# A decoder layer with 32 experts: 50 matrix products into an unread PSUM bank, between the output projection and the first expert

## The chip, the cores and the metric

The kernel runs on one NeuronCore of one Trainium2 chip. The metric is the device time of one execution in microseconds (us), the median of the runs shown. The engines are named as the profile names them: PE is TensorE (PEld its weight loads), DVE is VectorE, ACT is ScalarE, POOL is GpSimd, SP is SyncE. SP does no arithmetic here; it issues the large transfers from memory.

## The reference

One layer on 512 tokens of width 1024, float32:

```
p   = rmsnorm(x, g_mix) @ w_in          # q, k, v and three convolution inputs
mix = concat(rmsnorm(window_attention(q, k, v)), rmsnorm(short_conv(...)))
x   = x + mix @ w_out                   # the output projection
h   = rmsnorm(x, g_ffn)
logits = h @ w_router + b_router        # 32 experts; the top 4 of each token are used
act = clamped_swiglu(h[rows of expert e] @ w1[e] + b1[e])    # w1[e]: 1024 x 2048
y   = act @ w2[e] + b2[e]                                    # w2[e]: 1024 x 1024
x   = x + sum over the 4 experts of gate * y
out = rmsnorm(x, g_final)
```

The weights of the 32 experts are 12 MiB each in float32. They are all read once.

## The kernel before, in words

The 512 tokens are four tiles (t = 0 to 3) of 128. The work before the experts keeps them as rows or as columns of 128x128 blocks; the experts then take up to 96 rows each, gathered from memory by an index list (a "big" block: 64 rows at full width, 32 more as four quarters; `KINDS`, line 48, says which of the 32 places are big; places 0 and 1 are).

**The order of PE's work** is written out by hand in one list (lines 744 to 762 and on), and PE executes it strictly in that order; each step waits for semaphores of other engines. The stretch that matters here is:

- `out_proj(t, n)` (line 681): the output projection of tile t, column half n, into banks 0 and 1 (even t) or 2 and 3 (odd t). DVE adds the result to X in `residual` (line 1125).
- `turn_h2(t)` (line 707): eight 128x128 transposes of X into banks 4 and 5 (recorded at line 523, the helper's). ACT copies bank 4 to SBUF and DVE bank 5 (`turned_h2`, lines 1554 and 1146).
- `router(t)` (line 716): the logits, eight products of 32 columns that the trace shows as 16 instructions (line 728), into bank 6 or 0. DVE's `select(t)` (line 1151) takes the top four and marks the chosen experts.
- `rank(t)` (line 732): counts, for each token, how many earlier tokens chose the same expert. After `rank(3)` DVE's `place` (line 1173, timed at line 1184) compares ranks for the first two experts, and 16 products of one column (line 768) give the token lists of experts 0 and 1. DVE turns these to integers (line 1216), and POOL's indirect transfer fetches expert 0's rows (`fetch`, lines 1786 to 1789).
- Lines 772 and 773 count the tokens of each expert; DVE sorts the experts by count; lines 775 to 777 (after `sort_ready`) spread the order over partitions; lines 779 and 780 (after `nb_ready`) make prefix sums for overflow blocks.
- `turn_block(0)` (line 804) waits for expert 0's rows and transposes them (`turn_lines`, line 786). ACT copies them to `rowsT` (line 1603). Then `expert_blocks(compute)` runs the 32 experts.

DVE, ACT and POOL have hand-written orders of their own. DVE's order in this stretch is: select(0), select(1), residual(3,1), turned_h2(2), second_norm(3), place(0,2), turned_h2(3), select(2), select(3), place(2,4), the integer lists, the gates, the sort, the copies, and `list_entries` (line 1253). When `list_entries` is done, POOL writes the sorted list of all rows to memory by 16 indirect transfers (line 1814), reads it back (lines 1819 to 1821), and from it fetches the rows of expert 2 and every later one (line 1780).

**An expert** (`compute(i)`, line 899) is on PE: `first_product(i)` (w1, line 884: eight bias products on lines 834 and 837, then line 846 for the 64 rows and line 853 for the four quarters, in two groups of four slots), then, for i = 1, `turn_act_of(0)`, then `turn_block(i + 1)`, then `second_product(i - 1)` (w2, lines 859 to 878), then `turn_act_of(i)`. So `turn_block(2)`, which needs expert 2's rows, stands ahead of expert 0's second product. Every product reads its weights from a ring of 16 slots of 1 MiB.

**SP's order** fills the ring: eight loads of 2 MiB early (`load_first`, lines 450 to 465, the last one after expert 0's rows are in), then one load after another, each waiting (`wait_free`, line 430) until PE has used up the slots that it overwrites. The first of these needs the first group of expert 0's first product done; the w1 loads of place 3 need the first half of expert 0's second product.

`bias_sel` (96 x 2 x 128) and `bias_split` (96 x 3072), both bfloat16, are the operands of the bias products. `B_BOTH` (line 256) is bank 1.

Of the kernel before, what the change touches and what calls it, by code (L numbers as in the profile page):

```python
# [74 lines left out]
def layer_kernel(nc, x, g_mix, w_in, conv_w, sinks, g_attn_out, g_conv_out, w_out,  # L75
                 g_ffn, w_router, b_router, w1, b1, w2, b2, g_final, out):
    ctx = ExitStack()
    with ctx:
        def sb(name, shape, dt=F32):
            return ctx.enter_context(nc.sbuf_tensor(name, shape, dt))  # L80
# [5 lines left out]
        def sem(name):  # L86
            return ctx.enter_context(nc.semaphore(name))
# [42 lines left out]
        bias_split = sb("bias_split", [3 * E, 2 * FF + D], BF16)  # L130
        expert_sel = sb("expert_sel", [3 * E, E], BF16)
        bias_sel = sb("bias_sel", [3 * E, 2, P], BF16)
# [57 lines left out]
        ps = ctx.enter_context(nc.psum_tensor("ps", [P, 8, 512], F32))  # L190
# [65 lines left out]
        B_GLU, B_BOTH, B_LIN, B_Y, B_T = 0, 1, 2, 4, 6  # L256
# [11 lines left out]
        consts_ready, alibi_ready, biases_ready = sem("consts_ready"), sem("alibi_ready"), sem("biases_ready")  # L268
# [27 lines left out]
        cur_copied, cur_ready = sem("cur_copied"), sem("cur_ready")  # L296
# [43 lines left out]
        def fetches(upto):  # L340

            return 16 * sum(2 if BIG[i] and i >= STATIC else 1 for i in range(upto + 1))
# [7 lines left out]
        def expert_blocks(run):  # L350

            for i in range(E):
                run(i, i % 2)
# [163 lines left out]
        def _(pe):  # L517
            mm = pe.matmul

            def turn_rows(src, bank):  # L520

                for k in range(KT):
                    ins = pe.transpose(ps[:, bank + k // 4, (k % 4) * P:(k % 4 + 1) * P],
                                       src[:, k * P:(k + 1) * P], ident[:, :])
                return ins
# [155 lines left out]
            def out_proj(t, n, amid=None):  # L681

                if n == 0:
                    pe.wait_ge(mix_lo, t + 1)
                elif t == 0:
                    pe.wait_ge(wout_lo, KT)
                pe.wait_ge(x2_half, n * TB + t - 1)
                for k in range(KT):
                    if amid and k == CT:
                        amid()  # L690
                    bank, high, low, w_high, w_low = out_parts(t, n, k)
                    mm(bank, high, w_high, start=(k % CT == 0), stop=False)
                    mm(bank, high, w_low, start=False, stop=False)
                    ins = mm(bank, low, w_high, start=False, stop=(k % CT == CT - 1))
                ins.then_inc(oproj_done, 1)
# [11 lines left out]
            def turn_h2(t):  # L707
                pe.wait_ge(x2_half, TB + t + 1)
                if t == 0:
                    pe.wait_ge(gstd_ready, 1)  # L710
                else:
                    pe.wait_ge(h2T_a, t)
                    pe.wait_ge(h2T_b, t)
                turn_rows(X[:, t, :], 4).then_inc(h2_turned, 1)

            def router(t):

                pe.wait_ge(h2T_a, t + 1)
                pe.wait_ge(h2T_b, t + 1)
                if t == 0:  # L720
                    pe.wait_ge(wrt_ready, 1)
                elif t == 1:
                    pe.wait_ge(x2_half, 2 * TB - 1)
                else:
                    pe.wait_ge(chosen_ready, t - 1)
                logits = ps[:, LOGIT_BANKS[t % 2], 0:E]
                for k in range(KT):
                    ins = mm(logits, xnT[:, k, t * P:(t + 1) * P], w_rt[:, k, :],
                             start=(k == 0), stop=(k == KT - 1))
                ins.then_inc(logits_done, 1)  # L730

            def rank(t):

                pe.wait_ge(chosen_ready, t + 1)
                if t == 0:
                    pe.wait_ge(consts_ready, 2)
                if t == 2:
                    pe.wait_ge(pick_ready, 2 * t)
                own = ps[:, 7, t * E:(t + 1) * E]
                ins = mm(own, earlier[:, :], chosen[:, t, :], start=True, stop=(t == 0))  # L740
                if t:
                    ins = mm(own, ones_bf[:, :], chosen_cum[:, t, :], start=False, stop=True)
                ins.then_inc(rank_done, 1)
# [6 lines left out]
            out_proj(1, 1)  # L750
            turn_h2(0)
            out_proj(2, 1, lambda: router(0))
            turn_h2(1)
            out_proj(3, 1, lambda: router(1))
            turn_h2(2)
            router(2)
            rank(0)
            rank(1)
            turn_h2(3)
            router(3)  # L760
            rank(2)
            rank(3)

            pe.wait_ge(pick_ready, 2 * TB)
            for e in range(2):
                for t in range(TB):
                    for part in range(2):
                        ins = mm(ps[:, 5, e:e + 1], pick[:, e, t, :], tok_value[:, t, part:part + 1],
                                 start=(t == 0 and part == 0), stop=(t == TB - 1 and part == 1))
            ins.then_inc(tok_summed, 1)  # L770

            mm(ps[0:E, 4, 0:1], chosen_cum[:, TB, :], ones_bf[:, 0:1], start=True, stop=True)
            mm(ps[0:E, 4, E:2 * E], ones_bf[:, 0:E], chosen_cum[:, TB, :], start=True, stop=True).then_inc(counts_done, 1)
            pe.wait_ge(sort_ready, 1)
            mm(ps[0:1, 5, 2 * E:3 * E], expert_no[:, :], in_place[:, :], start=True, stop=True)
            mm(ps[0:3 * E, 5, 3 * E:4 * E], ident_bf[:, :, :].rearrange("e s f -> e (s f)"), in_place[:, :], start=True, stop=True)
            mm(ps[:, 5, 4 * E:6 * E], ones_bf[0:E, :], diag[:, :, :].rearrange("e s f -> e (s f)"), start=True, stop=True).then_inc(order_done, 1)
            pe.wait_ge(nb_ready, 1)
            mm(ps[0:OVF_ROWS, 4, 6 * E:7 * E], ovf_nb16[:, :], upto[:, :], start=True, stop=True)
            mm(ps[0:OVF_ROWS, 4, 7 * E:8 * E], ovf_nb16[:, :], ident_bf[:, 0, :], start=True, stop=True).then_inc(prefix_done, 1)  # L780
# [2 lines left out]
            def turn_lines():  # L783

                for k in range(KT):
                    ins = pe.transpose(ps[:, B_T + k // 4, k % 4 * MANY:(k % 4 + 1) * MANY],
                                       gathered[0:MANY, k * P:(k + 1) * P], ident[0:MANY, 0:MANY])
                ins.then_inc(rows_turned, 1)

            def turn(src, big, done):  # L790

                for c in range(6 if big else 4):
                    ins = pe.transpose(ps[:, B_T + c // 4, c % 4 * P:(c % 4 + 1) * P], src[:, c * P:(c + 1) * P], ident[:, :])  # L793
                ins.then_inc(done, 1)
# [9 lines left out]
            def turn_block(i):  # L804

                pe.wait_ge(rows_in, fetches(i))
                if i == 1:
                    pe.wait_ge(rows_ready, 2)
                elif i:
                    pe.wait_ge(actT_ready, 2 * (i - 1))  # L810
                if i < STATIC:
                    turn_lines()
                else:
                    turn(gathered, BIG[i], rows_turned)
# [97 lines left out]

            pe.wait_ge(biases_ready, 2)
            turn_block(0)
            expert_blocks(compute)
            pe.wait_ge(lin_ready, E)
            second_product(E - 1, 1, B_GLU)
# [476 lines left out]
        def _(act):  # L1394
# [17 lines left out]
            def high_tile(m):  # L1412

                if m == 0:
                    act.wait_ge(qkv_in, 16 * KT // 2)
                elif 2 <= m < QKV_TILES:
                    act.wait_ge(proj_done, m - 1)
                elif m == QKV_TILES:
                    act.wait_ge(conv_in, 16 * KT)
                    act.wait_ge(proj_done, QKV_TILES)  # L1420
                elif m >= QKV_TILES + 6:
                    act.wait_ge(part_done, 3 * ((m - QKV_TILES) // 3 - 1))
                raw, _, high = weight_tile(m)
                a.activation(high, raw, ACT.Copy).then_inc(tile_hi, 1)  # L1424
# [477 lines left out]
```

## Time and profile before

| | |
|---|---|
| three runs, median (lowest to highest) | 1236.43 us (1236.21 to 1237.57) |
| the profiled execution, its time | 1236.09 us |
| the profiled execution, its span | 1234.5 us |
| PE busy | 1158.3 us, 94% of the span |
| DVE / ACT / POOL busy | 25% / 16% / 14% |
| moved by DMA | 454.39 MB, mean 368 GB/s |
| weights on SP's queue | 434.16 MB, 84.7% of 16 engines' span |

Times in rows are microseconds from the span's start. In a timeline row the columns are: start, length, engine, line, operation, output<-inputs, shape, xcount, and in brackets the idle time before it with what ended it. Products on PE are pipelined: a row of one product is longer than the distance to the next start. In a row of windows, "PEclk" is the clock that TensorE was granted, as a share of full speed (1.00 is 2.4 GHz, 0.50 is 1.2 GHz), followed by the DMA engines' busy share and GB/s; "busy (x)" is busy time and the number of instructions.

### The profile page before, as it was taken

The numbers are of one execution on the slowest core, as the hardware profiler recorded it, in microseconds if no ns is written. First come the engines' busy times: TensorE is split into PE (matmuls) and PEld (weight loads), VectorE is DVE, ScalarE is ACT, GpSimd is POOL, SyncE is SP. The second block draws the span as 40 slices with busy tenths as digits, with TensorE's granted clock in tenths as the row PEclk, the third lists the DMA queues.
The fourth block names the chain that finished last, engine by engine and source line by source line (L and its number), as shares of the span: only waits on it lengthen the run. The fifth ranks groups of instructions, "written<-read, shape, count | busy, mean of one in ns | idle before, by whom it ended". The sixth has DMA issues, their size and how long they took to land. (4 is left out here: it accounts for less than half of the span.)

```text
span 1234.5 us, 16405 instructions
## 1 busy us (share of the span) xinstructions
PE 1158.3 (94%) x7022; PEld 481.7 (39%) x7022; DVE 306.6 (25%) x484; ACT 191.7 (16%) x378; POOL 174.2 (14%) x250
## 2 busy tenths in 40 slices
PE   5999998799999999999999999999999999999980
PEld 4777787223333333333333333333333333333330
DVE  4677756421111010101101010110101011010117
ACT  4453422011100101001100000110000010100002
POOL 6000100432101111110111111111111111111000
PEclk9999998799999999999999999999999999999996
DMA  9400675599999999999999999999999999999996
GB/s 336 148 1 3 224 309 214 173 368 404 426 426 425 426 429 423 426 425 429 424 425 425 427 427 424 427 426 427 423 426 427 426 425 427 426 425 427 427 383 235
DMA packets 51147, 454.39 MB, mean 368 GB/s; under 512 B 13044, under 2 KB 13316, under 8 KB 26400
## 3 DMA queue, kind: packets, MB, share of 16 engines
q1 hardware_dynamic: 42864, 434.16, 84.7%
q0 software_dynamic: 7632, 17.05, 3.6%
q10 hardware_dynamic: 576, 2.10, 0.4%
q8 instruction: 57, 0.93, 0.3%
q14 instruction: 18, 0.15, 0.0%
HBM read 442.60 MB, written 15.12 MB: 371 GB/s over the span
## 5 line engine op out<-in xcount | busy, mean ns | idle before, releaser
L846 PE MATMUL ps<-ring_a,blockT 128*64 128x512 f32 x1472 | 326.6, 597 | 8.5 <-DMA ring_a<-in_w 8.5
L1307 DVE TENSOR_SCALAR xnT<-ps 128x768 f32<-128x768 f32 (+1 forms) x32 | 26.9, 841 | 814.8 <-PE ps L853 516.1
L846 PEld LDWEIGHTS ps<-ring_a,blockT 128*64 128x64 f32 x1472 | 102.4, 137 | 218.5 <-issue 199.9
L872 PE MATMUL ps<-ring_a,actT 128*64 128x512 f32 x736 | 165.3, 596 | 0.8 <-DMA ring_a<-in_w 0.8
L846 PE MATMUL ps<-ring_b,blockT 128*64 128x512 f32 x448 | 99.5, 595 | 5.8 <-DMA ring_b<-in_w 5.8
L1594 ACT ACTIVATE blockT<-ps 128x512 f32<-128x512 f32 x30 | 17.9, 597 | 553.9 <-PE ps L793 553.9
L1780 POOL DMA_INDIRECT scores<-h_rows,slots x30 | 31.6, 1055 | 506.4 <-PE ps L793 505.5
L853 PE MATMUL ps<-ring_a,blockT 128*32 128x512 f32 x768 | 91.5, 615 | 0.0
L872 PEld LDWEIGHTS ps<-ring_a,actT 128*64 128x64 f32 x736 | 49.9, 136 | 93.6 <-issue 89.6
L1796 POOL DMA_INDIRECT expert_rows<-normed,slots x32 | 33.4, 1044 | 269.0 <-ACT normed L1623 268.7
L872 PE MATMUL ps<-ring_b,actT 128*64 128x512 f32 x288 | 64.7, 596 | 0.0
L846 PEld LDWEIGHTS ps<-ring_b,blockT 128*64 128x64 f32 x448 | 30.9, 137 | 69.9 <-issue 59.2
L878 PE MATMUL ps<-ring_a,actT 128*32 128x256 f32 x832 | 50.3, 382 | 0.0
L853 PEld LDWEIGHTS ps<-ring_a,blockT 128*32 128x32 f32 x768 | 21.9, 108 | 66.2 <-issue 66.2
L539 PE MATMUL ps<-xnT_hi,ring_r 128*128 128x512 f32 x144 | 39.8, 422 | 4.4 <-ACT ring_r L1424 2.3
L1329 DVE TENSOR_TENSOR xnT<-xnT 128x512 f32<-128x512 f32 (+1 forms) x50 | 42.9, 915 | 4.2 <-ACT xnT L1617 3.6
L878 PEld LDWEIGHTS ps<-ring_a,actT 128*32 128x32 f32 x832 | 24.4, 109 | 34.5 <-issue 21.1
L543 PE MATMUL ps<-xnT_lo,ring_r 128*128 128x512 f32 x144 | 36.1, 393 | 0.0
L546 PE MATMUL ps<-xnT_hi,ring_r 128*128 128x512 f32 x144 | 35.6, 389 | 0.0
L1622 ACT ACTIVATE normed<-ps,slots 128x256 f32<-128x256 f32 x18 | 8.5, 474 | 173.2 <-PE ps L878 173.2
L1623 ACT ACTIVATE normed<-ps,slots 128x512 f32<-128x512 f32 x32 | 21.9, 684 | 81.8 <-PE ps L872 81.8
L872 PEld LDWEIGHTS ps<-ring_b,actT 128*64 128x64 f32 x288 | 20.0, 136 | 35.9 <-issue 35.0
(300 smaller groups left out, 1069.0 us busy)
## 6 DMA issues: line engine op xcount, KB each, us to landing
ring_a<-in_w SPq DMA_DIRECT2D x144, 2048.0 KB, 30.0
ring_b<-in_w SPq DMA_DIRECT2D x48, 2048.0 KB, 31.6
ring<-in_w_in SPq DMA_DIRECT2D x12, 768.0 KB, 19.0
ring<-expert_rows SPq DMA_DIRECT2D x16, 512.0 KB, 14.0
X<-in_x SPq DMA_DIRECT2D x8, 512.0 KB, 6.5
ring<-in_w_out SPq DMA_DIRECT2D x8, 512.0 KB, 4.6
h_rows<-normed ACTq DMA_DIRECT2D x4, 512.0 KB, 3.6
out<-ring SPq DMA_DIRECT2D x4, 512.0 KB, 2.6
```

The source lines that it names most:

```text
L539: mm(ps[:, bank, :], high[:, k, :], xnT_hi[:, k, :], start=(k == 0), stop=False)
L543: mm(ps[:, bank, :], high[:, k, :], xnT_lo[:, :, k, :], start=False, stop=False)
L546: ins = mm(ps[:, bank, :], low[:, k, :], xnT_hi[:, k, :], start=False, stop=(k == KT - 1))
L846: ins = mm(ps[half * HALF:(half + 1) * HALF, b, :], x_of(k)[0], ring(r)[:, 0, at + half * 512:at + (half + 1) * 512], start=False, stop=(k ...
L853: mm(ps[q * QUARTER:(q + 1) * QUARTER, B_BOTH, :], x_of(k)[1], quarter_cols(w, q), start=False, stop=(k == KT - 1), tile_position=(0, q * ...
L872: ins = mm(ps[half * HALF:(half + 1) * HALF, bank, :], actT[:, s % 2 * W2_K + j, s // 2 * HALF:(s // 2 + 1) * HALF], ring(r)[:, 0, j * D + ...
L878: ins = mm(ps[q * QUARTER:(q + 1) * QUARTER, bank + 1, 0:256], actT[:, 4 + j, s * QUARTER:(s + 1) * QUARTER], ring(slot(s)[0])[:, 0, j * D ...
L1307: v.tensor_scalar(width(glu_c, big), width(ps_glu, big), LIMIT, None, ALU.min).then_inc(glu_ready, 1)
L1329: ins = v.tensor_tensor(turned.rearrange("p (k q) -> p q k", k=n), a_in.rearrange("p (q k) -> p q k", k=n), b_in.rearrange("p (q k) -> p q ...
L1623: a.activation(gated_y[:, parity, 0:512], ps[:, bank, :], ACT.Copy, scale=gates[:, HALVES, 1:2].bitcast(F32)).then_inc(y_ready, 1)
L1780: g.indirect_dma_start(gathered[:, 0:512], None, h2_halves, bass.IndirectOffsetOnAxis(lists[:, HALVES, 0:1], 0), bounds_check=last_half_to ...
L1796: g.indirect_dma_start(y_halves, bass.IndirectOffsetOnAxis(slots[:, HALVES, i, 0:1], 0), gated_y[:, parity, 0:512], None, bounds_check=las ...
```

## The change

A helper on PE issues a number of products of 96 x 128 by 96 x 512 in bfloat16, all of them into bank 1, each starting a new sum. Nobody reads the bank before the first expert's own bias products start it anew. Seven calls are put between steps of PE's list, 6 + 3 + 8 + 5 + 16 + 8 + 4 = 50 products; ahead of the first stand two waits, for the operands.

```diff
+            def keep_busy(count):
+
+                for _ in range(count):
+                    mm(ps[:, B_BOTH, :], bias_sel[:, 0, :], bias_split[:, 0:512], start=True, stop=True)
+
...
             turn_h2(2)
+            pe.wait_ge(biases_ready, 2)
+            pe.wait_ge(cur_ready, 2)
+            keep_busy(6)
             router(2)
             rank(0)
             rank(1)
             turn_h2(3)
+            keep_busy(3)
             router(3)
             rank(2)
+            keep_busy(8)
             rank(3)
+            keep_busy(5)
 
             pe.wait_ge(pick_ready, 2 * TB)
...
             mm(ps[0:E, 4, E:2 * E], ones_bf[:, 0:E], chosen_cum[:, TB, :], start=True, stop=True).then_inc(counts_done, 1)
+            keep_busy(16)
             pe.wait_ge(sort_ready, 1)
...
+            keep_busy(8)
             pe.wait_ge(nb_ready, 1)
...
             pe.wait_ge(biases_ready, 2)
             turn_block(0)
+            keep_busy(4)
             expert_blocks(compute)
```

## Rows read from the trace of the kernel before

**Rows 1.** The page's slices (40 equal parts): TensorE's clock, in tenths.
```profile
PEclk9999998799999999999999999999999999999996
```
**Rows 2.** Windows, the stretch 400 to 1200; after PEclk come DMA share and GB/s.
```profile
400.00:1200.00 800.00, 784.08 (x4948) 264.95 (x4946) 98.25 (x132) 78.24 (x150) 103.33 (x104) 1.00 1.01 425
```
**Rows 3.** PE's timeline near the end of the weights.
```profile
1181.12 3.65 PE L846 MATMUL ps<-ring_a,blockT 128*64 128x512 f32 x16 [1.19 <-DMA ring_a<-in_w]
```
**Rows 4.** SP's timeline from 225 to 290: issues of weight loads.
```profile
237.78 2.13 SPq L428 DMA_DIRECT2D ring_a<-in_w  x2
...
283.72 5.77 SPq L423 DMA_DIRECT2D ring_a<-in_w  x2
```
**Rows 5.** PE's timeline from 196 to 236.
```profile
201.73 0.39 PE L694 MATMUL ps<-ring_r,mixer_r 128*128 128x512 f32 x1
201.96 1.03 PE L523 MATMUL ps<-ident,X 128*128 128x128 f32 x8
204.40 1.94 PE L728 MATMUL ps<-w_rt,xnT 128*128 128x32 f32 x16 [1.40 <-ACT xnT L1556]
...
206.25 1.81 PE L523 MATMUL ps<-ident,X 128*128 128x128 f32 x8
208.90 3.59 PE L728 MATMUL ps<-w_rt,xnT 128*128 128x32 f32 x16 [0.83 <-ACT xnT L1556]
...
214.56 0.21 PE L740 MATMUL ps<-chosen,earlier 128*128 128x32 bf16 x1 [2.02 <-DVE chosen_cum L1165]
...
215.96 0.59 PE L768 MATMUL ps<-tok_value,pick 128*128 128x1 bf16 x16 [1.16 <-DVE pick L1184]
...
220.49 0.18 PE L775 MATMUL ps<-in_place,expert_no 32*1 32x32 bf16 x1 [3.79 <-DVEq L1235]
...
222.72 0.20 PE L779 MATMUL ps<-upto,ovf_nb 32*32 32x32 bf16 x1 [1.80 <-DVE ovf_nb L1242]
...
222.88 1.54 PE L786 MATMUL ps<-ident,scores 96*128 96x96 f32 x8
225.44 1.06 PE L834 MATMUL ps<-bias_split,bias_sel 96*64 96x512 bf16 x4 [1.02 <-ACT rowsT L1603]
```
**Rows 6.** Windows of half a microsecond: PE busy, its clock, DMA share, GB/s.
```profile
206.00:206.50 0.50, 0.50 (x9) 0.92 1.07 459
...
230.00:230.50 0.50, 0.50 (x4) 0.69 0.10 41
```
**Rows 7.** PE's timeline from 225 to 290: expert 0's first product, then expert 1's.
```profile
226.98 8.72 PE L846 MATMUL ps<-ring_a,rowsT 128*64 128x512 f32 x32
...
250.13 0.88 PE L786 MATMUL ps<-ident,scores 96*128 96x96 f32 x8
252.38 0.62 PE L834 MATMUL ps<-bias_split,bias_sel 96*64 96x512 bf16 x4 [1.37 <-DVE xnT L1312]
...
253.28 7.09 PE L846 MATMUL ps<-ring_a,rowsT 128*64 128x512 f32 x32
```
**Rows 8.** DVE's timeline: the copy of bank 5 for router(3).
```profile
208.10 0.69 DVE L1148 COPY xnT<-ps 128x512 f32<-128x512 f32 x1 [0.28 <-PE ps L523]
```
**Rows 9.** POOL's timeline from 250 to 300: the fetch of expert 2's rows.
```profile
267.37 1.14 POOL L1780 DMA_INDIRECT scores<-h_rows,slots  x1 [0.89 <-POOL slots L1827]
```
**Rows 10.** The fetched rows' tile, 262 to 300: two fetches' landing.
```profile
DMA to landing us min/median/max: 8.5/8.6/8.7
```
**Rows 11.** PEld's timeline, 274 to 278: weight load needing expert 2's rows.
```profile
276.75 0.42 PEld L793 LDWEIGHTS ps<-ident,scores 128*128 128x128 f32 x4 [1.26 <-DMA scores<-h_rows,slots]
```
**Rows 12.** DMA issues, 274.5 to 277 (load of 275.07): KB, us to landing.
```profile
ring_b<-in_w SPq DMA_DIRECT2D x1, 2048.0 KB, 12.7
```
**Rows 13.** PE's timeline from 0 to 150: the first products, the last attention block.
```profile
16.76 1.97 PE L523 MATMUL ps<-ident,normed 128*128 128x128 f32 x8 [0.62 <-DVE normed L953]
21.06 3.75 PE L539 MATMUL ps<-xnT_hi,ring_r 128*128 128x512 f32 x8 [2.32 <-ACT ring_r L1424]
...
147.83 1.95 PE L605 MATMUL ps<-probsT,mixer 128*64 128x256 f32 x16 [0.83 <-issue]
```

## Prediction, made before the changed kernel ran

> **What bounds the kernel now.** I read the page's clock slices first, then the windows, then PE's timeline between the output projection and the first experts, and last SP's and POOL's timelines behind it. The slices [rows 1] show full clock but for two dips before the end (the start, too, ran at the lower level by the length of its products [rows 13], which this line does not show); only the second, in slices 7 and 8 (about 185 to 247 us), lies where the change works. From 400 to 1200 us the DMA engines are wholly busy at 425 GB/s while PE idles 16 of 800 us [rows 2], and near the end of the weights PE still waits for its ring [rows 3]. So the end of the run is set by when the stream of expert weights gets going, not by how fast PE is afterwards. The stream stands nearly still before 237.78, when SP issues the first load that had to wait for slots freed by expert 0 [rows 4]: the DMA share at 230 is 0.10 [rows 6]. Whatever brings PE's early work forward brings that load forward.
>
> PE's timeline there [rows 5] is a chain of short steps with gaps, each gap ended by DVE or ACT. The clock falls to 0.50 inside 206.0 to 206.5 (mean 0.92, so at about 206.4) and returns inside 230.0 to 230.5 (mean 0.69, so at about 230.3) [rows 6]. What went before the fall: 1.40 us idle and 1.94 us of router products with 32 columns. What went before the return: five microseconds of dense products from 225.44. Between the two PE pays twice per step where PE itself is the cost: router(3) takes 3.59 where router(2) took 1.94, the eight transposes at 206.25 take 1.81 where those at 201.96 took 1.03 [rows 5].
>
> **What the change costs and gives, step by step.** Price of a filler: two starts of full-array products of 512 columns are 0.23 apart at full clock (201.73 to 201.96 [rows 5]); eight at the lower level take 3.75, 0.47 each [rows 13]. The trace has no bfloat16 product of 96 rows by 128 columns; I take 0.23, with 0.47 as the other end. Weight loads of such products run beside the products before, so I count none.
>
> The two added waits cost nothing: ACT waited for the biases before it split the output weights, and POOL raised cur_ready before it added the squares that the group sums need. Both lie upstream of the output projection. Nothing new is issued on SP or POOL, and no queue is passed.
>
> Do the fillers fit, at 0.23? Six take 1.38 in a gap of 1.40; router(2) is not delayed. Three take 0.69 after transposes that end near 207.3, and router(3) cannot start before 208.6 (below). Eight take 1.84 in a wait of 2.02; five 1.15 in 1.16; sixteen 3.68 in 3.79; eight 1.84 in 1.80; four 0.92 in 1.02 [rows 5]. All are covered within 0.05, the cover being DVE's selection, its comparison, its sort, and ACT's copy. If the clock is not held every one but the first three sticks out (a rival below).
>
> If it is held, the gains add up along one chain. (1) The transposes at 206.25 end 0.78 sooner, but DVE was idle only 0.28 before its copy [rows 8], because it placed the first experts before: router(3) starts 0.28 sooner. (2) router(3) takes 1.94 in place of 3.59: 1.65. So DVE's last selection, rank(3), expert 0's list, the sort and list_entries all move by 1.93; that part of DVE's work is back to back and does not shrink. (3) Expert 0's transposes take 0.88 as expert 1's do, not 1.54: 0.66. (4) Its bias products take 0.90 from 252.38 to 253.28, not 1.54 from 225.44 to 226.98: 0.64. (5) Its first 32 products take 7.09, not 8.72: 1.63 [rows 5, 7]. Sum 4.86: the load of 237.78 would go out near 232.9.
>
> That is not what reaches the end. Expert 2's rows come by the index list, and POOL's chain starts at DVE's list_entries, so the fetch at 267.37 [rows 9] moves only by the 1.93, to 265.4. It takes 8.6 to land [rows 10]: 276.0 before, 274.0 after. PE took up those rows at 276.75 [rows 11], 0.75 after they landed, because ACT was late too. With PE 4.86 ahead, ACT is no longer late and the fetch is: PE goes on at about 274.1, a gain of 1.93 + 0.7 = 2.6. What is queued behind this wait is expert 0's second product, whose first half frees the slots for the load of 283.72 [rows 4]. The load before it went out at 275.07 and landed 12.7 later, at 287.8 [rows 12], so that of 283.72 was issued 4.1 before the stream ran out. Moved by 4.9 and 2.6 these become 282.9 and 281.1: 1.8 ahead. That leaves the DMA engines short for a moment, and the stream is then tied to PE's 2.6. From there everything up to the end moves along at 425 GB/s.
>
> Bounds: 1.9, if the 0.75 after landing stays or the list's small transfers land later among weights that now run beside them; 4.9, if the lead in the stream is kept. I take 2.6, since the load of 283.72 stands behind the wait in PE's own order. The profiled execution took 1236.09 and lies 0.34 below the median; against the median 1236.43 - 2.6 = 1233.8. A measurement of this kernel can tell about 0.2%, 2.5 us, from no change: the forecast stands just at that line.
>
> **The rivals.**
> *The lead is kept (8%).* If the stream does not run short near 282, the whole 4.9 reaches the end: 1231.5. For it: 1.8 us are left between issue and end of the load before. Against it: the later loads follow PE too.
>
> *The clock falls once all the same (18%).* Its place is 206.3 to 209.8: transposes, three fillers, a wait for DVE, part of router(3). Against a fall: in the last attention block transposes, 0.83 of idle time and products of 256 columns stood together and those products still ran at full speed, 16 in 1.95 [rows 13]. For it: at the start of the kernel four rounds of eight transposes, the last at 16.76, took 1.97 each, twice the 1.03 of later, and the clock came up only in the dense products after 21.06 [rows 5, 13]; transposes don't raise it. The Trainium skill (TensorE: Matmul & The Clock Gate, Part 4: PE-mode transpose) says that transposes don't count as TensorE being busy in the way products do; the rows of the start agree. By that rule the stretch is mostly unbusy and this rival would be the likelier. Its price: router(3) ends about 0.7 later than forecast, the eight fillers run partly at 0.47 and delay rank(3) by some 0.8, and the dense fillers bring the clock back. The list gains 0.4, PE's take-up of expert 2's rows 1.1: 1235.3, within 0.2%.
>
> *The fillers come too late (10%), slower.* If the clock falls at 206.4 as before and stays low, fillers cost 0.47: three end at 209.5 (router(3) 0.6 late, ending 213.1), eight at 216.9 (rank(3) 2.3 late), five at 219.5 (the lists 3.5 late), sixteen at 227.8 where the order was wanted at 224.0, the last eight at 231.8: the prefix sums, and with them list_entries, 9 us late: 1245. It decides only if the clock is still low when the sixteen start. As the clock came back after five microseconds of dense products before [rows 5, 6], a middle case is likelier, with only rank(3) and the lists late, by 2.5: 1238.5 to 1239.5, slower by about 0.2%.
>
> *Nothing comes of it (4%).* The stream turns out limited elsewhere, or the fillers hold nothing: 1236.4.
>
> **How the numbers follow.** The forecast itself gets 60%; its own range is 1232.5 to 1235.0, and some two thirds of it lie beyond 2.5 us: 0.40. With the kept lead's 0.08 that is 0.48 for faster. Within 0.2%: 0.20 of the forecast, 0.18 and 0.04, and a little of the late fillers: 0.43. Slower: 0.09. The range 1231.2 to 1237.0 takes in the kept lead in part, the forecast and the single fall, and leaves out the late fillers and what is below.
>
> **What would show it.** Right: clock 1.00 throughout 203 to 240; router(3) in about 1.95 and ended near 210.6; the fillers 0.23 apart; rank(3) near 212.6 and the lists near 214.0, each released by DVE and not by a filler; the first load after the standstill near 233, POOL's fetch of expert 2 near 265.4, and PE idle about 2 us for these rows near 272 to 274. Wrong: a clock of 0.50 in 207 to 216 (a fall), fillers directly ahead of rank(3) or line 775 with no idle time (they are late), or a DMA stream that stays 5 us ahead beyond 290 (the lead is kept).

## The result, and the profile of the changed kernel

The changed kernel takes 1244.41 us (median of 6 runs, 1241.64 to 1246.44), the kernel before 1236.34 (6 runs, 1233.49 to 1237.84, among them the three shown for it above): ratio 1.0066, 95% interval 1.0052 to 1.008. It is 8 us slower. The forecast was 1233.8, in a range up to 1237.0. The profiled execution took 1246.44, the longest of the six; its span is 1244.8 where the one before had 1234.5, so 10.3 us are to be found between the two traces.

First the stretch that the change works on. PE's timeline of the changed kernel; L719 are the fillers, and lines behind them are 5 to 13 higher than before (L733 is the router's, L745 rank, L779 the first experts' lists, L787 and L792 the two sort steps, L799 expert 0's rows, L847 and L859 its first product):

```profile
203.50 1.46 PE L719 MATMUL ps<-bias_split,bias_sel 96*128 96x512 bf16 x6
205.07 1.95 PE L733 MATMUL ps<-w_rt,xnT 128*128 128x32 f32 x16
...
206.93 1.07 PE L523 MATMUL ps<-ident,X 128*128 128x128 f32 x8
207.84 0.81 PE L719 MATMUL ps<-bias_split,bias_sel 96*128 96x512 bf16 x3
209.21 1.94 PE L733 MATMUL ps<-w_rt,xnT 128*128 128x32 f32 x16 [0.56 <-ACT xnT L1570]
...
211.12 3.41 PE L719 MATMUL ps<-bias_split,bias_sel 96*128 96x512 bf16 x8
214.32 0.23 PE L745 MATMUL ps<-chosen,earlier 128*128 128x32 bf16 x1
...
215.75 0.55 PE L779 MATMUL ps<-tok_value,pick 128*128 128x1 bf16 x16
...
220.26 0.17 PE L787 MATMUL ps<-in_place,expert_no 32*1 32x32 bf16 x1 [0.26 <-DVEq L1249]
...
222.49 0.18 PE L792 MATMUL ps<-upto,ovf_nb 32*32 32x32 bf16 x1
...
222.63 0.88 PE L799 MATMUL ps<-ident,scores 96*128 96x96 f32 x8
...
224.53 0.62 PE L847 MATMUL ps<-bias_split,bias_sel 96*64 96x512 bf16 x4 [0.16 <-ACT rowsT L1617]
...
225.42 7.09 PE L859 MATMUL ps<-ring_a,rowsT 128*64 128x512 f32 x32
```

Against [rows 5, 7]: router(3) takes 1.94, not 3.59; expert 0's transposes 0.88, not 1.54; its bias products 0.89 (224.53 to 225.42), not 1.54; its first 32 products 7.09, not 8.72. All that was forecast for PE is there, with one exception: the eight fillers at 211.12 take 3.41. The windows of half a microsecond (PE busy, its clock, DMA share, GB/s) show why:

```profile
211.00:211.50 0.50, 0.50 (x6) 0.81 0.64 270
...
214.50:215.00 0.50, 0.50 (x6) 0.78 1.39 573
```

The clock fell at about 211.3 and came back at about 214.7; before, it was low from 206.4 to 230.3 [rows 6]. DVE had the last choice of experts ready at 213.16:

```profile
212.99 0.17 DVE L1179 TENSOR_TENSOR chosen_cum<-chosen_cum,chosen 128x32 bf16<-128x32 bf16 x1
```

but rank(3) came at 214.32, 1.2 later, behind the fillers. So the list gained next to nothing (231.68 below, 231.74 before). SP's first weight load after the standstill did; SP's timeline:

```profile
234.64 2.13 SPq L428 DMA_DIRECT2D ring_a<-in_w  x2
245.55 16.03 SPq L423 DMA_DIRECT2D ring_a<-in_w  x4
270.06 2.14 SPq L428 DMA_DIRECT2D ring_b<-in_w  x2
294.00 13.92 SPq L423 DMA_DIRECT2D ring_a<-in_w  x4
```

It went out at 234.64, 3.1 sooner than at 237.78, while the load that went out at 283.72 [rows 4] now goes out at 294.00, 10.3 later: exactly what the span grew by. The whole loss therefore lies between 234 and 294. POOL's timeline in that stretch:

```profile
231.68 1.03 POOL L1828 DMA_INDIRECT slot_list<-entry,row_i  x1 [6.93 <-DVE entry L1295]
...
260.10 1.16 POOL L1833 DMA_DIRECT2D slots<-slot_list  x2 [7.71 <-DMA slot_list<-entry,row_i]
261.21 2.02 POOL L1835 DMA_DIRECT2D slots<-slot_list  x4
273.66 0.29 POOL L1840 TENSOR_SCALAR slots<-slots,half_col 128x32 int32<-128x32 int32 x1 [10.42 <-DVE slots L1350]
...
275.88 1.45 POOL L1794 DMA_INDIRECT scores<-h_rows,slots  x1 [0.89 <-POOL slots L1841]
```

The sixteen writes of the list begin at 231.68; its six read-backs go out at 260.1 to 263.2; and then POOL waits 10.42 us. In the kernel before the same rows were:

```profile
231.74 1.03 POOL L1814 DMA_INDIRECT slot_list<-entry,row_i  x1 [6.08 <-DVE entry L1281]
...
258.99 1.16 POOL L1819 DMA_DIRECT2D slots<-slot_list  x2 [7.05 <-DMA slot_list<-entry,row_i]
260.11 2.02 POOL L1821 DMA_DIRECT2D slots<-slot_list  x4
...
265.13 0.29 POOL L1826 TENSOR_SCALAR slots<-slots,half_col 128x32 int32<-128x32 int32 x1 [3.01 <-DVE slots L1336]
```

The DMA issues of 256 to 262 (count, KB each, median us from issue to landing), first before, then changed:

```profile
slots<-slot_list POOLq DMA_DIRECT2D x4, 8.0 KB, 2.7
slots<-slot_list POOLq DMA_DIRECT2D x2, 16.0 KB, 3.2
```

```profile
ring_a<-in_w SPq DMA_DIRECT2D x2, 2048.0 KB, 11.1
slots<-slot_list POOLq DMA_DIRECT2D x2, 16.0 KB, 6.6
slots<-slot_list POOLq DMA_DIRECT2D x2, 8.0 KB, 7.8
```

One by one the six read-backs of 8 and 16 KB take 6.5 to 10.6 us, the last one longest, where they took 2.4 to 3.3. What is different are two weight loads of 2 MiB each, the third and fourth w1 load of place 2. SP's timeline, the third load (before: the third and fourth), first before, then changed:

```profile
262.58 2.17 SPq L423 DMA_DIRECT2D ring_a<-in_w  x2
```

```profile
259.44 0.33 SPq L423 DMA_DIRECT2D ring_a<-in_w  x1
```

Before, the third load went out 1.0 us behind the last read-back (261.58); now it goes out ahead of all six. An earlier load, the second of place 2, is still under way beside the read-backs in both. Everything of expert 2 hangs on these read-backs. PE's timeline:

```profile
284.66 1.11 PE L806 MATMUL ps<-ident,scores 128*128 128x128 f32 x4 [12.13 <-DMA scores<-h_rows,slots]
...
286.61 5.23 PE L885 MATMUL ps<-ring_a,actT 128*64 128x512 f32 x16
```

PE stands 12.13 us for expert 2's rows and takes them up at 284.66 (before 276.75 [rows 11]). The 16 products behind them took 3.65 in the kernel before:

```profile
277.90 3.65 PE L872 MATMUL ps<-ring_a,actT 128*64 128x512 f32 x16
```

In the windows of the changed kernel, PE's clock falls during that wait, and DMA has run out of work:

```profile
276.00:280.00 4.00, 0.00 (x0) 0.00 (x0) 0.31 (x1) 0.00 (x0) 1.32 (x1) 0.52 0.98 416
280.00:284.00 4.00, 0.00 (x0) 0.00 (x0) 0.00 (x0) 0.00 (x0) 0.00 (x0) 0.50 0.63 262
284.00:288.00 4.00, 3.34 (x14) 1.49 (x16) 0.71 (x2) 1.33 (x2) 1.32 (x2) 0.50 0.08 13
288.00:292.00 4.00, 4.00 (x18) 1.05 (x18) 0.80 (x1) 0.00 (x0) 0.00 (x0) 0.77 0.16 55
```

The sum: read-backs issued 1.1 later (260.10 against 258.99) and read 7.4 more slowly make the fetch of expert 2's rows 8.5 late (275.88 against 267.37 [rows 9]); 0.6 of that falls into the slack there was, 7.9 reach PE; the four transposes, six bias products and 16 products at the lower clock add 2.4: 10.3 at the load of 294.00.

One thing is needed to read the experiments: in seven of the eleven profiles the clock falls at about 59 us (mean 0.84 from 55 to 66), in those of the third, fourth, sixth and seventh experiment it does not (1.00), and there all times of this stretch lie some 2 to 4 us sooner, so distances are compared inside one profile, and times by medians.

### The profile page after: what moved, and what is told of

Its sections match the earlier page's. It is cut to its first block and busy times, and to the rows that moved or that the text cites. A ratio compares the mean times of both kernels' runs of the same rounds, so it can differ in the third digit from the quotient of the medians.

```text
span 1244.8 us, 16506 instructions
## 1 busy us (share of the span) xinstructions
PE 1167.5 (94%) x7072; PEld 484.1 (39%) x7072; DVE 306.4 (25%) x484; ACT 191.5 (15%) x378; POOL 174.1 (14%) x250
## 5 line engine op out<-in xcount | busy, mean ns | idle before, releaser
L859 PE MATMUL ps<-ring_a,blockT 128*64 128x512 f32 x1472 | 325.2, 594 | 9.1 <-DMA ring_a<-in_w 9.1
L859 PEld LDWEIGHTS ps<-ring_a,blockT 128*64 128x64 f32 x1472 | 101.9, 137 | 218.2 <-issue 194.9
L859 PE MATMUL ps<-ring_b,blockT 128*64 128x512 f32 x448 | 99.8, 595 | 5.9 <-DMA ring_b<-in_w 5.9
L859 PEld LDWEIGHTS ps<-ring_b,blockT 128*64 128x64 f32 x448 | 30.8, 137 | 70.6 <-issue 58.6
L806 PE MATMUL ps<-ident,scores 128*128 128x128 f32 x152 | 23.6, 287 | 12.1 <-DMA scores<-h_rows,slots 12.1
```

The costliest lines, as they stand in the source:

```text
L859: ins = mm(ps[half * HALF:(half + 1) * HALF, b, :], x_of(k)[0], ring(r)[:, 0, at + half * 512:at + (half + 1) * 512], start=False, stop=(k ...
```

## The experiments

Theory A: the list's read-backs need a stretch in which no weight load runs beside them; the change brings the loads forward and not the list, and takes that stretch away. Theory B: the fillers themselves hold PE back. Theory C: something behind expert 2 is contended.

**The changed kernel with one wait more on SP.**

```diff
                     n = w1_slot(i, k)
+                    if i == 2 and k == 4:
+                        sp.wait_ge(slots_in, 16 * 6)
                     wait_free(n + 1)
```

> The changed kernel, with one wait more: SP holds the third of the four w1 loads for place 2 until the sorted list has been read back. Theory A (the weight loads that now go out about 3 us earlier run beside the list's six small read-backs, which then land after about 8 to 10 us and not 3, and everything from expert 2's rows on is late by that): the read-backs land in about 3 us again, the fetch of expert 2's rows goes out near 267 and not 276, PE's wait for them falls from 12 us to about 3, and the time falls from 1244 to 1234 to 1237. Theory B (the fillers themselves hold back rank(3), the list and PE): the wait changes nothing there, 1243 to 1245. Theory C (the loss is contention of PE, DVE or DMA somewhere after expert 2): no change either, 1243 to 1245.

Measured: 1235.51 (10 runs), ratio 1.0, interval 0.9982 to 1.0018. POOL's and PE's timelines:

```profile
264.51 0.29 POOL L1842 TENSOR_SCALAR slots<-slots,half_col 128x32 int32<-128x32 int32 x1 [1.61 <-DVE slots L1352]
...
266.73 1.14 POOL L1796 DMA_INDIRECT scores<-h_rows,slots  x1 [0.89 <-POOL slots L1843]
```

```profile
275.68 0.95 PE L808 MATMUL ps<-ident,scores 128*128 128x128 f32 x4 [3.06 <-DMA scores<-h_rows,slots]
...
277.47 4.55 PE L887 MATMUL ps<-ring_a,actT 128*64 128x512 f32 x16
```

The read-backs land in 1.7 to 1.9, POOL's wait falls from 10.42 to 1.61, PE's from 12.13 to 3.06, and the loss is gone. All 50 fillers are still there, so B and C fall. But nothing is won either: PE takes up the rows 1.1 sooner than before, and the clock, which falls at about 275.9, just after the 3.06 us of standing, takes it back (16 products in 4.55 where 3.65 were before).

**The first two calls alone.**

```diff
             turn_h2(2)
             pe.wait_ge(biases_ready, 2)
             pe.wait_ge(cur_ready, 2)
             keep_busy(6)
...
             turn_h2(3)
             keep_busy(3)
             router(3)
             rank(2)
-            keep_busy(8)
             rank(3)
-            keep_busy(5)
...
-            keep_busy(16)
...
-            keep_busy(8)
...
-            keep_busy(4)
```

> The changed kernel with the first two calls of the helper alone (6 and 3 products); the other 41 products are left out. router(3) then runs at full clock, and the list and the first weight load after the standstill both move forward by 1.5 to 2 us; the lead of the weights over the list stays that of the kernel before. Theory A: no collision, 1234 to 1236, and the fetch of expert 2's rows near 265.5. Theory B: nine fillers cost little by themselves, 1236 to 1238. Theory C: about 1237 to 1240, as the first expert is earlier too.

Measured: 1235.61 (10 runs), ratio 0.9999, interval 0.9981 to 1.0017. The list starts at 230.30 and the first load goes out at 235.86, 5.6 apart; the read-backs land in 2.1 to 2.4. No collision, as A has it. The time alone does not tell A from B (1236 to 1238); the landing does. The fetch goes out at 266.43, 0.9 later than expected.

**The kernel before, its list 3 us late.**

```diff
             pool.wait_ge(entries_ready, TB + 1)
+            for _ in range(12):
+                then(g.memset(ranks[:, :, :], 0.0))
             for t in range(TB):
```

> The kernel before, without any filler, but POOL fills a dead tile 12 times (about 3 us) between the list's entries and its first write to memory: the list is 3 us late against weight loads that stay where they are. Theory A: the read-backs now run beside the third and fourth w1 load of place 2 and land after 7 to 10 us; the fetch of expert 2's rows goes out at 275 to 279 where 267.4 was before, and the time is 1242 to 1247, far more than the 3 us put in. Theories B and C: 3 us of lateness at most, less the slack of 0.7 us: 1238 to 1240.

Measured: 1246.09 (4 runs), ratio 1.0093, interval 1.0059 to 1.0127: 10 us for 3.96 put in (the fills and their steps, 227.06 to 231.02). POOL's, DVE's and PE's timelines:

```profile
227.06 3.10 POOL L1813 MEMSET ranks<- 128x128 f32 x12 [5.27 <-DVE entry L1281]
231.02 1.04 POOL L1816 DMA_INDIRECT slot_list<-entry,row_i  x1 [0.86 <-POOL ranks L1813]
...
259.41 1.16 POOL L1821 DMA_DIRECT2D slots<-slot_list  x2 [7.95 <-DMA slot_list<-entry,row_i]
```

```profile
272.15 0.20 DVE L1336 TENSOR_SCALAR slots<-slots 128x64 int32<-128x64 int32 x1 [20.50 <-DMA slots<-slot_list]
```

```profile
283.93 1.11 PE L793 MATMUL ps<-ident,scores 128*128 128x128 f32 x4 [12.26 <-DMA scores<-h_rows,slots]
```

Without a single filler this is the changed kernel's trace: the list starts 2.7 ahead of the first load (231.02 to 233.72), the third load (258.52) goes out ahead of the first read-back, the read-backs take 6.4 to 10.1, PE stands 12.26. The fetch goes out at 274.77, 12.1 later than in the profile of the fourth experiment (262.71), which like this one is without the fall at 59. This shows A from the other side.

**The kernel before with the wait on SP.** The edit is that of the first experiment, on the kernel before.

> The kernel before with the same wait on SP. The control for e1_gate: the list's read-backs landed in about 3 us there already, at 264.7, and the load that is held went out at 262.6. Theory A: the load goes out 2 us later and the rest stays: 1235.5 to 1238. Theories B and C: the same. If it comes out well below 1235, the list and the weights collide in the kernel before too.

Measured: 1235.89 (10 runs), ratio 1.0002, interval 0.9986 to 1.0018. The wait costs nothing and gives nothing measurable by itself; what it gave in the first experiment came from the collision that it prevents.

**The wait, and five fillers in place of three.**

```diff
             turn_h2(3)
-            keep_busy(3)
+            keep_busy(5)
             router(3)
```

> e1_gate with five products in place of three after the transposes of turn_h2(3). In e1_gate the clock fell at about 211 with the eight products still to come, these then took 3.55 us in place of 1.9, rank(3) came at 214.3 and the list no sooner than before (231.7). If the three products were too few to hold the clock: it stays at 1.00 from 203 on, rank(3) comes near 213, the list starts near 230.4, the fetch of expert 2's rows goes out near 265.3, and the time is 1 to 2 us under e1_gate, 1233.5 to 1235. If the clock falls in any case, the run equals e1_gate, 1235 to 1236.5.

Measured: 1235.11 (12 runs), ratio 0.9991, interval 0.9976 to 1.0007. The clock stays at 1.00 from 200 to 274 and the eight fillers take 1.89; the list starts at 230.30, the fetch goes out at 265.41, as expected. PE still stands 1.85 us for the rows, and the 16 products behind it take 5.35: the clock falls at 276 there again.

```profile
275.43 5.35 PE L887 MATMUL ps<-ring_a,actT 128*64 128x512 f32 x16
```

The median is 0.4 below the first experiment's, where 1 to 2 were expected, and not clear of no change.

**Ten more fillers ahead of that wait, into a bank free at that time.** The edit is on the fifth experiment.

```diff
+                if i == 1:
+                    pe.wait_ge(ovf_ready, 1)
+                    for _ in range(10):
+                        mm(ps[:, B_Y + 1, :], bias_sel[:, 0, :], bias_split[:, 0:512], start=True, stop=True)
                 if i < E - 1:
                     turn_block(i + 1)
```

> e5_gate_five with ten more products, into bank 5, directly ahead of the wait for expert 2's rows. In e1_gate PE stood 3.06 us there, the clock fell to 0.50 at 276, and the first 16 products of expert 0's second product took 4.55 us in place of 3.65: of the 1.07 us by which PE took up the rows sooner nothing was left at the next weight load (284.18; 283.72 in the kernel before). If that fall is what eats the rest: the clock stays at 1.00 there, the 16 products take 3.65, and the time is about 1 us under e5_gate_five. If the stream's end is set elsewhere, no difference.

Measured: 1233.08 (12 runs), ratio 0.9976, interval 0.9962 to 0.9991. PE's timeline:

```profile
269.56 2.32 PE L921 MATMUL ps<-bias_split,bias_sel 96*128 96x512 bf16 x10
271.72 0.60 PE L808 MATMUL ps<-ident,scores 128*128 128x128 f32 x4
...
272.81 3.65 PE L887 MATMUL ps<-ring_a,actT 128*64 128x512 f32 x16
```

The ten fill the wait, the clock holds, the 16 products take 3.65. This version is faster than both kernels, by 0.24% of the kernel before. Its median is 2.0 below the fifth experiment's, where about 1 was expected. Inside the profiles 1.2 of it is seen: from the fetch of expert 2's rows to the next weight load pass 17.5 us in the fifth (265.41 to 282.94) and 16.3 here (262.33 to 278.63). The rest is not shown, and the two intervals overlap.

**The list 1 us late.** The edit of the third experiment with 4 fills in place of 12.

> The kernel before with the list 1 us late (4 fills of a dead tile in place of 12 in e3_list_late). In the kernel before the last read-back landed at 264.7 and the third w1 load, issued at 262.6, began to move data at about 265: by theory A the margin is about 0.3 us, so 1 us is enough for the last of the six read-backs to meet the load, and the cost is well over 1 us: 1238 to 1245. If the collision grows in step with the overlap (no edge): 1236.5 to 1238.

Measured: 1236.84 (10 runs), ratio 1.0011, interval 0.9988 to 1.0034. The median misses what A expected and lies in the range of the other reading, that the collision grows in step with the overlap. But the ten runs, of which three lie between 1231 and 1233, have two at 1242.71 and 1242.96, above the highest of the 29 runs of the kernel before that ran beside them (1240.89). The profiled execution has no collision: the list starts 4.7 ahead of the first load, the last read-back goes out 0.8 ahead of the third load, and the read-backs land in 2.6 to 3.4. So the margin is not the 0.3 us that I read from one trace: with the list 1 us late most executions get through.

**Five fillers, clock held, no wait on SP.** The edit of the fifth experiment, on the changed kernel.

> The changed kernel with five products in place of three after the transposes of turn_h2(3), and no wait on SP: the clock is held, as the prediction's likeliest case had it, and nothing else is mended. The list then starts about 4.2 us ahead of the first weight load after the standstill, where it was 6.0 in the kernel before, 3.0 in the changed one. Theory A (the list needs a lead over the weights, and the changed kernel takes it away): a lead of 4.2 still lets the last read-backs meet the third w1 load in most runs: median 1238 to 1244, spread wide. If the fall of the clock and the late rank(3) were the cause: 1233 to 1235.

Measured: 1241.74 (9 runs, 1232.78 to 1246.78), ratio 1.0051, interval 1.0031 to 1.0072. The run at 1232.78 is the profiled one; the other eight lie from 1239.04 up. In the profile the clock is at 1.00 from 203 to 240, and the list starts 3.7 ahead of the first load. Its third load and its last read-back, in SP's and POOL's timelines:

```profile
258.86 0.33 SPq L423 DMA_DIRECT2D ring_a<-in_w  x1
```

```profile
258.87 0.54 POOL L1835 DMA_DIRECT2D slots<-slot_list  x1
```

The five read-backs ahead of the load land in 2.8 to 3.6; the sixth, 0.01 behind it, takes 6.1. The fetch goes out at 267.61, 2.2 later than in the fifth experiment, but lands in 5.2 where it takes 8.4 to 9.1 in the other ten profiles, so PE is not held up for it. So the very case that the prediction held likeliest, the change with a clock that does not fall, is slow too in eight of nine executions; that the clock held in those eight was not seen.

**The read-backs on ACT's queue.** The edit is on the sixth experiment (five fillers, ten more ahead of expert 2), whose wait on SP is left out; the six read-backs move from POOL's queue to ACT's (the lines taken out of POOL's order are not shown).

```diff
                 sigmoid(i, BIG[i])
+                if i == 0:
+                    read_back()
...
+            def read_back():
+
+                list_rows = list_dram.rearrange("(r e) w -> r (e w)", e=E)
+                in_sbuf = slots[:, :, :, :].rearrange("p b e w -> p b (e w)")
+                act.wait_ge(list_written, 16 * (1 + TB * TOPK))
+                for h in range(2):
+                    act.dma_start(in_sbuf[h * HALF:(h + 1) * HALF, HALVES, :], list_rows[0:HALF, :]).then_inc(slots_in, 16)
+                for q in range(4):
+                    act.dma_start(in_sbuf[q * QUARTER:(q + 1) * QUARTER, QUARTERS, :], list_rows[HALF:MANY, :]).then_inc(slots_in, 16)
```

> e6_gate_six without the wait on SP; instead the six read-backs of the list are issued by ACT, after its work for expert 0, and not by POOL. If the read-backs land late because small transfers on POOL's queue stand behind the weights, another queue may land them in 3 us among the weights: 1232 to 1234. If every small transfer is late beside two 2 MiB loads, whatever the queue: they land after 6 to 10 us and the time is 1238 to 1244.

Measured: 1244.08 (11 runs), ratio 1.0061, interval 1.0043 to 1.008. The move does not help. Whether the queue matters this does not decide: the profiled execution is the shortest of the eleven (1236.22) and shows no collision, so how long the read-backs take in the ten longer ones was not seen. The edit also spreads the six issues over 4.5 us (257.24 to 261.71) where POOL takes 2.6, which by itself would bring the last ones nearer to the third load. In the profile that load was late (262.65), as the clock fell at 224.5 and the first load went out 5.9 behind the list's start.

**Across the eleven profiles.** How long a read-back takes goes by whether it is issued ahead of the third w1 load of place 2. Those ahead of it land in 1.7 to 3.7 us (all six in the kernel before and the experiments other than the third and eighth, five of six in the eighth); those behind it in 6.1 to 10.6 (all six in the changed kernel and the third experiment, one in the eighth). The first experiment moves the load behind the read-backs and the third the read-backs behind the load, and each time the landing follows.

## Why the prediction was wrong, step by step

- **What bounds the kernel: right.** The shift of the load of 283.72, 10.3, is the shift of the span. The slices [rows 1] show one dip before the end, though, not two: the fall at 59 is too short for them. Nothing in the sum hangs on it.
- **The fillers' price: right.** Six take 1.46 and router(2) is not late: 1.41 lie between the transposes and it, 1.40 before [rows 5].
- **The gains on PE, steps 2 to 5: right** to 0.05 each. That the first load moved by 3.1 and not 4.9 has two causes: the late fillers ahead of rank(3) (1.2), and a stretch that starts 0.7 later in this profile (the transposes of tile 2 at 202.63, before 201.96).
- **That the clock is held: wrong in the profiled run.** It fell once, in 211.3 to 214.7; this is the rival of a single fall, a little later than placed. By that rival the list was to gain 0.4; it starts 0.06 sooner, or 0.7 counted from the transposes of tile 2. The Trainium skill (TensorE: Matmul & The Clock Gate, Part 4: PE-mode transpose) says that transposes don't count as TensorE being busy in the way products do. No run here shows whether transposes are to blame for this fall: with two products more beside the same transposes the clock stayed at 1.00 from 203 to 224 in all four profiles with five fillers.
- **The step that failed** is the one from the earlier first load to the end: "the fetch at 267.37 moves only by the 1.93", with "the list's small transfers land later among weights that now run beside them" as a bound on the gain, worth 0.7. I saw that the weights would gain 3 us on the list, and priced it as a smaller gain. It is a loss: read-backs of 2.4 to 3.3 become 6.5 to 10.6, and 13.2 us pass from the first one's issue to DVE's use (260.10 to 273.26) where 5.7 did (258.99 to 264.73). The fetch at 267.37 moves by 8.5 the other way, to 275.88. The rows that would have told it stood in the trace: the last read-back went out at 261.58, 1.0 ahead of the third load, between two pairs of loads. The forecast moved the loads 4.9 and the list 1.9, which puts the third load at about 257.7 among read-backs issued from 257.1 to 259.7, and it kept the landing times of the gap.
- **The rival on the slow side had the wrong mechanism.** It had 1245 for fillers that come too late at the lower clock; that 1244.41 was measured beside it is chance. Such lateness there was (rank(3), 1.2), but the first experiment removes the loss with all fillers in place, and the third makes it with none.
- **"PE idle about 2 us for these rows"** came out as 12.1, and "DMA short for a moment" as a stream at a share of 0.17 from 283 to 296.

What stays open: why a small transfer issued behind the third load is late, whether its queue has a part in that, and what happens in the long executions of the seventh, eighth and ninth experiment, none of which was profiled.

## What to carry to other kernels

When a change brings a stream of large transfers forward, look for the small transfers that used to fall into the gap ahead of it, above all those that a chain of index lists waits for: here their landing time went by whether they were issued ahead of the large load, not by their size. Compare the two issue times as the change would shift them, and price a lost lead as a loss of its own sign, by the landing time of the same kind of transfer under load. A wait that holds the large load until the small ones are in cost nothing measurable here (ratio 1.0002 on the kernel before), and the one version that is clearly faster than the kernel before (0.9976) has it.

## What the hardware showed that was not expected

- Transfers of 8 and 16 KB land in 1.7 to 3.7 us when they are issued ahead of the third load of 2 MiB, and in 6.1 to 10.6 when they are issued behind it. The Trainium skill (Trainium Kernel Development and Optimization, Key Constraints) says that transfers from the SP, ACT and POOL queues run on the same 16 DMA engines and interleave. The changed kernel's trace agrees: from 266 to 272, where five of the six read-backs land, the profile counts 3.0% of the 16 engines' time for POOL's queue and 99.2% for SP's.
- Whether the clock falls differs between executions of one and the same stretch. From 55 to 66 us its mean is 0.84 in the profile of the kernel before and 1.00 in that of the fourth experiment, whose code there is the same; that execution took 1230.73 where the median of its version is 1235.89. The windows (PE busy, its clock, DMA share, GB/s), before and fourth experiment:

```profile
55.00:66.00 11.00, 8.93 (x45) 0.84 0.01 2
```

```profile
55.00:66.00 11.00, 9.00 (x53) 1.00 0.01 2
```

- PE's clock fell at 275.9, 0.2 us after PE had stood 3.06 us for expert 2's rows (first experiment), and at 276.0, 1.7 us after it had stood 1.85 us for them (fifth); with ten products without use in that wait it stayed at 1.00 (sixth).
